# Toeplitz matrices of an S5 layer made by TensorE instead of DMA, and gate products moved ahead

## What is computed

```python
def s5_mix(u, h0r, h0i, ...):
    ...
    bu_r = jnp.einsum('btgc,gpc->btgp', uf, bbr)
    bu_i = jnp.einsum('btgc,gpc->btgp', uf, bbi)
    ...
    pr, pim, hr, hi = lax.associative_scan(_ssm_combine, (a_r, a_i, bu_r, bu_i), axis=1)
    ...
    y = (jnp.einsum('btgp,gcp->btgc', hr, c_re.astype(F32))
         - jnp.einsum('btgp,gcp->btgc', hi, c_im.astype(F32)))
    y = y.reshape(bsz, t, SEQ_WIDTH) + d_skip.astype(F32) * u.astype(F32)
    y = jax.nn.gelu(y).astype(u.dtype)
    y = y * jax.nn.sigmoid(y @ w_glu + b_glu)
```

## Time and profile before

| | |
|---|---|
| device time, median of 3 runs | 1501.69 us (1501.1 to 1504.21) |
| device time of the profiled execution | 1501.93 us |
| its span, first to last instruction | 1499.9 us |
| PE busy / PEld busy | 1408.9 us (94%) / 1309.3 us (87%) |
| DVE / ACT / POOL busy | 954.8 / 576.3 / 638.5 us |
| mean granted TensorE clock | 0.975 |

### The profile page before, as it was taken

How to read it: one execution, slowest core, us unless ns; L and a number is a source line. 1 busy time by engine, 2 the same in 40 slices (tenths; PEclk the granted TensorE clock), 3 DMA queues, 4 the chain that set the end, 5 groups by cost and what they waited for, 6 DMA issues and landing times.

```text
span 1499.9 us, 33629 instructions
## 1 busy us (share of the span) xinstructions
PE 1408.9 (94%) x12665; PEld 1309.3 (87%) x12665; DVE 954.8 (64%) x1623; ACT 576.3 (38%) x1025; POOL 638.5 (43%) x417
## 2 busy tenths in 40 slices
PE   6987868989999999999899989999999999999998
PEld 6985658979999999999889965557899999999997
DVE  5779867577773177765658688653676761377755
ACT  4554354354342134322434245431454431234323
POOL 1599322304343344442269878302214344344441
PEclk9997889999999999999999999999999999999999
DMA  6363364223333223333236669994222333223321
GB/s 175 110 139 67 66 167 127 84 59 86 98 99 99 75 84 98 91 97 91 66 109 192 204 189 313 325 328 148 75 69 85 93 96 91 84 88 94 105 83 64
DMA packets 289087, 180.55 MB, mean 120 GB/s; under 512 B 54248, under 2 KB 274572, under 8 KB 288924
## 3 DMA queue, kind: packets, MB, share of 16 engines
q1 hardware_dynamic: 288412, 179.07, 41.0%
q10 hardware_dynamic: 576, 0.13, 0.0%
HBM read 167.10 MB, written 10.63 MB: 118 GB/s over the span
## 4 chain that ended last, share of the span: by engine, by line
PE 74%; DVE 12%; issue 4%; ACT 3%; SPq 2%; DMA 2%; POOL 2%; DVEq 0%; ACTq 0%; POOLq 0%
PE big L2824 56%; PE big L2906 3%; PE misc L3021 2%; SPq L633 2%; DVE y L1869 1%; PE misc L3527 1%; DVE x L1878 1%; DVE x_lo L1320 1%; PE misc L3161 1%; PE misc L3278 1%; PE misc L3166 1%; PE misc L2891 1%; ACT w_hi L2280 1%; POOL w_lo L988 1%; PE big L2938 1%
## 5 line engine op out<-in xcount | busy, mean ns | idle before, releaser
L988 POOL TENSOR_TENSOR w_lo<-raw,w_hi 128x1024 fp32r<-128x1024 f32 (+2 forms) x150 | 387.0, 2580 | 701.7 <-ACT w_hi L2280 472.8
L2280 ACT ACTIVATE w_hi<-raw 128x1024 fp32r<-128x1024 f32 (+2 forms) x173 | 192.1, 1111 | 568.2 <-PE big L2824 536.1
L2824 PE MATMUL big<-x_hi,w_hi 128*128 128x264 f32 x1984 | 406.0, 286 | 4.7 <-DVE x_lo L1318 1.6
L2824 PE MATMUL big<-x_hi,w_lo 128*128 128x264 f32 x1984 | 400.2, 283 | 0.0
L2824 PE MATMUL big<-x_lo,w_hi 128*128 128x264 f32 x1984 | 398.2, 282 | 0.0
L2824 PEld LDWEIGHTS big<-x_hi,w_hi 128*128 128x128 f32 x1984 | 305.1, 188 | 9.5 <-issue 3.5
L2824 PEld LDWEIGHTS big<-x_lo,w_hi 128*128 128x128 f32 x1984 | 304.9, 188 | 0.0
L2824 PEld LDWEIGHTS big<-x_hi,w_lo 128*128 128x128 f32 x1984 | 304.7, 188 | 0.0
L1966 DVE SCALAR_TENSOR_TENSOR yc<-uc,convw,yc 128x512 f32<-128x512 f32 x88 | 136.7, 1553 | 113.2 <-ACT yc L2679 113.2
L2824 PE MATMUL big<-h_hi,w_hi 128*128 128x264 f32 x616 | 124.9, 284 | 6.3 <-DVE h_lo L1981 6.3
L2824 PE MATMUL big<-h_lo,w_hi 128*128 128x264 f32 x616 | 123.9, 282 | 0.0
(11 more groups left out here) (463 smaller groups left out, 2307.6 us busy)
## 6 DMA issues: line engine op xcount, KB each, us to landing
raw<-in_w_up SPq DMA_DIRECT2D x88, 512.0 KB, 3.8
raw<-in_w_down SPq DMA_DIRECT2D x32, 704.0 KB, 4.6
areas<-in_cache_k SPq DMA_DIRECT2D x41, 384.0 KB, 4.2
areas<-in_cache_v SPq DMA_DIRECT2D x41, 384.0 KB, 4.6
raw<-in_w_in SPq DMA_DIRECT2D x16, 512.0 KB, 4.4
raw<-in_w_out SPq DMA_DIRECT2D x16, 512.0 KB, 4.3
raw<-in_w_kv SPq DMA_DIRECT2D x12, 512.0 KB, 4.4
spare<-in_cache_k SPq DMA_DIRECT2D x12, 384.0 KB, 4.4
```

Of the source, the lines that this page charges most:

```text
L988: pool.tensor_tensor(w_lo[slot][:, 0:kb, :], raw[slot][:, 0:kb, :], w_hi[slot][:, 0:kb, :].bitcast(F32), ALU.subtract).then_inc(lo_made, 1)
L2280: A.activation(w_hi[slot][:, 0:kb, :], raw[slot][:, 0:kb, :], ACT.Copy).then_inc(hi_made, 1)
L2824: ins = pe.matmul(big[2 * slot + b_][:, 0:c1 - c0], w[slot][:, k, :], r[:, c0:c1], start=(k == 0 and n_ == 0), stop=(k == kb - 1 and n_ == 2))
```

## The change

1. `bb_wide` (in the idle `qrow` tile) holds each `bb` matrix with 16 zero columns on either side. With it as the stationary, TensorE forms all eight block rows of the Toeplitz matrix directly in the bank: for each 32 rows two products (odd and even block row), each as wide as the row is filled. The bank is first cleared by a product with a zero tile. ScalarE reads 128 x 512 in place of 16 x 512 straight into `toep`; `kern`, its 24 transfers and the zeroing of `toep` are gone. There are two `toep` tiles.
2. The output sums of third 0 move from third 1 to the end of third 0, ahead of head step 2. `u_load(2)` and the returns of y follow at their own waits.
3. The split parts of k = 0 to 3 go to tiles of their own (`glu_hi`, `glu_lo`), are made among the memory samples, and the products of these k for the first two panels stand right behind the output sums and the head turns, ahead of `fin_turns`. `w_lo` of these panels moves from VectorE to GpSimd, the last two adds of z from GpSimd to VectorE. Panel 2 has weight tiles of its own (`third`). The memory values (`mv0`) lie under `x_hi` and `x_lo` now, are loaded in two halves behind the load of the fourth weight panel, and `gate_in(0)` waits until they are used.

```diff
-        jobs += [("Y", 0, a) for a in range(TG // 4) if t == 1]
...
-        jobs += [("Y", 1, a) for a in range(TG // 4) if t == 1]
+        jobs += [("Y", t, a) for a in range(TG // 4) if t + 1 < THIRDS]
     for a in range(0, TG // 4, 2):
         jobs += [("mq", 0, a + b) for b in range(2)] + [("Y", THIRDS - 1, a + e) for e in range(2)]
-    jobs += [("fin", ri) for ri in range(2)] + [("OT", 0, p) for p in LAST[0]]
-    jobs += [("mq", 0, b) for b in range(TG // 4, NB)]
...
-        toep = a("toep", [P, TG, P])
+        toep = [a("toep0", [P, TG, P])]
...
-        kern = a("kern", [CH, TG, P])
+        toep.append(a("toep1", [P, TG, P]))
+        bb_wide = qrow[:, 0:2 * TP * 3 * CH].rearrange("p (r j n) -> p r j n", r=2, n=3 * CH)
...
+        third = [nc.alloc_sbuf_tensor_at(f"third_{nm}", [P, KS, P], F32R, offset=bp_end + 4 * KS * P * n)
+                 for n, nm in enumerate(("hi", "lo"))]
...
-        mb = [dict(v=a("mv0", [P, NB, 2, NMEM]), prod=a("mprod0", [P, 2, NMEM]), s_flat=a("ms0", [P, 2 * NB * MEMH + 32]),
+        glu_hi, glu_lo = (a(f"glu_{nm}", [P, KS - 2, NT], F32R) for nm in ("hi", "lo"))
+        mv0 = [nc.alloc_sbuf_tensor_at(f"mv0_{n}", [P, HALF_B, 2, NMEM], F32, offset=x_hi_at + 4 * KD * NT * n)
+               for n in range(2)]
+        mb = [dict(v=[mv0[b // HALF_B][:, b % HALF_B] for b in range(NB)], prod=a("mprod0", [P, 2, NMEM]), s_flat=a("ms0", [P, 2 * NB * MEMH + 32]),
...
-                if 0 < t < THIRDS - 1:
-                    sp.wait_ge(s_("b_used"), t + 1)
-                    sp.wait_ge(s_("cT_made"), t + 1)
-                    bc_load(t + 1)
-                if t == 1:
-                    full(sp, ("Y", 0, 3))
-                    y_store(0)
-                elif t == 2:
-                    y_return(0)
-                    full(sp, ("Y", 1, 3))
-                    y_store(1)
-                    full(sp, ("bT", 2, 3))
-                    for b in range(MK_EARLY + 1):
-                        mem_k(b)
-                    y_return(1)
-                sp.wait_ge(s_("s5_zero"), 2)
-                sp.wait_ge(s_("kern_ready"), 4 * (t + 1))
-                for tau in range(CHUNK):
-                    load(toep[CH * tau:CH * tau + CH, :, (CHUNK - 1 - tau) * CH:P],
-                         kern[:, :, 0:(tau + 1) * CH], "toep_in")
-                if t == 1:
-                    u_load(2)
-
+            sp.wait_ge(s_("b_used"), 2)
+            sp.wait_ge(s_("cT_made"), 2)
+            bc_load(2)
+            y_store(0)
+            full(sp, ("Y", 0, 3))
+            u_load(2)
+            y_return(0)
...
+            for b in range(MK_EARLY + 1):
+                mem_k(b)
...
+            def beside_glu(i):
+
+                if i != 3:
+                    return
+                sp.wait_ge(s_("yz_used"), THIRDS - 1)
+                for n in range(2):
+                    mem_v(0, mv0[n], slice(HALF_B * n, HALF_B * n + HALF_B))
+                sp.wait_ge(s_("hout_ready"), 2)
...
+            weights("glu", cols(I["w_glu"][0]), beside_glu, start=2)
...
-                        own.tell(pool.memset(toep[:], 0.0), s_("s5_zero"), 2)
-                        own.tell(pool.memset(qrow[:], 0.0), s_("s5_zero"), 3)
+                        own.tell(pool.memset(qrow[:], 0.0), s_("s5_zero"), 2)
+                        own.tell(pool.memset(zeros[:], 0.0), s_("s5_zero"), 3)
...
+                if name == "glu":
+                    for i in range(n):
+                        if i == 3:
+                            pool.wait_ge(lo_made, base + 3)
+                        if i != 2:
+                            lo(base + i, (base + i) % 2, kb)
+                    continue
...
+
+            def add_z_tile(m):
+
+                k = 2 * THIRDS - 2 + m
...
+                    dve.wait_ge(s_("yz_in"), 16 * THIRDS)
+                    dve.wait_ge(s_("yz_used"), THIRDS - 1)
+                do(V.tensor_tensor(y[:, k, :], y[:, k, :], yz_last[:, m, :], ALU.add))
+                sync()
+                mark(s_("yz_used"))
+
...
-            for b in range(4):
+            for b in range(2):
                 mem_sample(0, mb[0], b)
+            dve.wait_ge(s_("hfin_made"), THIRDS)
+            for k in range(2):
+                glu_split(k)
+            for b in range(2, 4):
+                mem_sample(0, mb[0], b)
+            for k in range(2, KS - 2):
+                glu_split(k)
+            for b in range(4, 6):
+                mem_sample(0, mb[0], b)
+            for p in LAST[0]:
+                head_lo(0, p)
+            for m in range(2):
+                add_z_tile(m)
+            glu_split(KS - 2)
             for ri in range(2):
                 full(dve, ("fin", ri))
                 freed(own, V.tensor_copy(hout[:, ri].rearrange("p a n -> p (a n)"),
                                          bank(("fin", ri))[0:108, 0:256]), ("fin", ri))
                 sync()
                 mark(s_("hout_ready"))
-            for p in LAST[0]:
-                head_lo(0, p)
...
-                    tell(V.tensor_tensor(o, srcv, h, ALU.subtract), s_("xlo_made"), stat[1] - 1 + c)
+            glu_split(KS - 1)
+            third_q = PH["glu"][2] + 2
+            dve.wait_ge(hi_made, third_q + 1)
+            dve.wait_ge(lo_made, third_q)
+            V.tensor_tensor(third[1][:], raw[third_q % 2][:, 0:KS, :], third[0][:].bitcast(F32),
+                            ALU.subtract).then_inc(lo_made, 1)
...
                 do(A.activation(y[:, k, :], y[:, k, :], ACT.Gelu_apprx_tanh))
 
+            act.wait_ge(s_("s5_zero"), 2)
             for t in range(THIRDS):
                 if t:
                     full(act, ("V", t - 1, 2))
                     input_copies(t)
-                if t == 1:
-                    read_y(0)
+                act.wait_ge(s_("b_used"), t + 1)
+                do(A.activation(bb_wide[:, :, :, CH:2 * CH], bb[t % 2][:], ACT.Copy))
+                mark(s_("bb_spread"))
...
                 for a_ in range(TG // 4):
-                    if t and a_ == 0:
-                        act.wait_ge(s_("toep_in"), 16 * CHUNK * t)
-                    read_bank(("K", t, a_), kern[:, same_side(a_)[0]:same_side(a_)[-1] + 1:2, :],
-                              bank(("K", t, a_))[0:CH, :].rearrange("p (g n) -> p g n", g=4))
-                    mark(s_("kern_ready"))
+                    read_bank(("K", t, a_), toep[t % 2][:, same_side(a_)[0]:same_side(a_)[-1] + 1:2, :],
+                              bank(("K", t, a_))[:].rearrange("p (g n) -> p g n", g=4))
+                    mark(s_("toep_ready"))
                 if t == 0:
...
                     for n in range(3, 6):
...
+            for k in range(2):
+                gelu(k)
+            sync()
+            act.wait_ge(s_("hp_ready"), THIRDS)
+            for k in range(2):
+                glu_in(k)
+            for k in range(2, KS - 2):
                 gelu(k)
             sync()
             read_y(THIRDS - 1, range(TG // 8))
+            for k in range(2, KS - 2):
+                glu_in(k)
...
+            for k in range(KS - 2, KS):
+                gelu(k)
+                sync()
                 glu_in(k)
+            act.wait_ge(raw_loaded[base % 2], ((base + 2) // 2 + 1) * 16)
+            A.activation(third[0][:], raw[base % 2][:, 0:KS, :], ACT.Copy).then_inc(hi_made, 1)
...
 
             def y_sums(t, between=None):
-                pe.wait_ge(s_("toep_in"), 16 * CHUNK * (t + 1))
...
             for t in range(THIRDS):
                 if t:
                     input_sums(t)
-                if t == 1:
-                    y_sums(0)
-                elif t == 0:
+                if t == 0:
                     pe.wait_ge(panel_read, PH["memkv1"][2] + 4)
                     scores(0, 0)
                     scores(0, 1)
+                    pe.wait_ge(s_("s5_zero"), 3)
                 pe.wait_ge(s_("cp_ready"), t + 1)
+                pe.wait_ge(s_("bb_spread"), t + 1)
                 for a_ in range(0, TG // 4, 2):
                     o = [take(("K", t, a_ + e)) for e in range(2)]
+                    for e in range(2):
+                        pe.matmul(o[e][:, :], zeros[:], ident_bf[:].unsqueeze(1).to_broadcast([P, 4, P]), start=True, stop=False)
                     for n in range(4):
                         for ri in range(2):
-                            for e in range(2):
-                                g = same_side(a_ + e)[n]
-                                r = slice(STATE * e, STATE * e + STATE)
-                                ins = pe.matmul(o[e][0:CH, n * P:n * P + P], bb[t % 2][r, ri, g // 2, :],
-                                                cp[t % 2][r, ri, g // 2, 0:P], start=(ri == 0), stop=(ri == 1))
-                                if n == 3 and ri == 1:
-                                    give(ins, ("K", t, a_ + e))
+                            for odd in (1, 0):
+                                for s in range(P // 32):
```

(66 more changed lines are left out.)

115 lines of the change are left out of this document (54 added, 61 removed).

## The result

The change makes the kernel slower. Four runs of the changed kernel took 1513.11 us in the median (1510.55 to 1519.69), four of the kernel before 1502.66 (1501.1 to 1504.21). The ratio is 1.0082, with a 95% interval of 1.0065 to 1.0100, so 12.3 us (10.5 between the medians). The forecast was 1496.6, the range 1490.5 to 1507. The time lies outside the range, on its slow side. The profiled execution of after is the slowest of its four (1519.69 us, span 1517.1, 17.2 over that of before), so its rows show some 7 us more than the median has.

The account below looks back on a forecast made before the run. A stage of dependences, no one engine the bound. +0.5 (last output bank), -6.1 (first two gate panels) and +0.5 (third) make -5.1 us on 1501.9: 1496.8, less 0.2 for the median, 1496.6 us; 80% range 1490.5 to 1507.

Parts of the forecast that it names:

- the price of the K sums: TensorE's new K sums: 8.5 us a third instead of 3.67, so +4.8 us (bounds +4.1 and +10.7).
- rival C: Slower: K records cost 25.6 ns each, 14.4 us a third, tiles not overlapped or engine underfed; 1508 us, chance 19%.
- First third: VectorE waits for scores behind the moved output sums; `cp` starts 6.2 us late, 2 more at low clock, taken as +7.5.
- Second and last third: Delay stays +7.5, last scan +3, `hp` at 203.4; ScalarE's queue then reads the last output bank at 217.2, +0.5 us.
- The 8.6 us of waiting are spent on dearer K sums: Before the last output bank: TensorE's removed waits for row loads are used up by costlier K, leaving +0.5 us.
- No wait for `toep`: Sign to look for on TensorE: its 8.6 us of waiting for the row loads disappears.
- Gate panels: Last output bank to first two finished panels: 13.3 us instead of 19.4, so -6.1 us (-5.4 to -6.8).
- Column maximum: Memory softmax behind the third gate panel: arrives 6 to 7.6 us after two panels, where 6.5 passed before; +0.5 us.
- the two terms: Last output bank to the memory softmax's column maximum: -6.1 us for the first two panels and +0.5 for the third.

Follow-up runs that it names:

- the loop: Changed kernel, three of four groups in each K bank run as one group repeated in a hardware loop (wrong sums): 1499.8 us, one run, beside 1496.9 before.
- the sums behind the third head step: Changed kernel with the first third's output sums behind the third head step, not ahead of it: ratio 1.0071; with K summed as before, 0.9984 (1498.7 us).
- the old K in the new order: Changed kernel with K summed as before, row loads included; moved output sums and gate-panel order kept: ratio 0.9968, 1497.9 us.
- the tail alone: Kernel before with only the change's last part, the early splits and first blocks of two gate panels: ratio 0.9968, 1496.8 us.
- the narrow: Changed kernel with every K product streaming 16 columns instead of 16 to 128 (K incomplete): 1518.4 us, one run, beside 1496.9 before.
- the placing products: Kernel before with only the gate-panel part, its row loads replaced by 32 selection-matrix products a third: ratio 1.0111, 1519.8 us.

## Why the prediction was wrong

**The step that failed is the first term, the price of the K sums**: 8.5 us a third, measured 13.5, 14.2 and 14.6. The working asked only whether the array overlaps its tiles. It does: 14.2 ns a record in the bursts, near the 17.5 of the earlier trace rows that I had leaned on, and 9.1 to 10.2 us for a third where the loop feeds it. What the sum left out is that 512 records with their weight loads are 1,024 instructions, four packets at 3.5 to 4 us each. The page of before gives instructions and packets; I read neither. I named the supply only inside rival C, whose price of 14.4 us was right (13.1 and 0.9 for the zeroing are 14.0; the rest is the changes of tile shape, which the text doesn't name there), and gave it 19%.

**Rival C** had the size of the term and too small a sum: 2 x 5.9 us in VectorE's chain, 1508. Measured was 1513.1. It missed that the last third's K delays the last output sums too (it ends at 224.8, 5.1 us behind `hp`), and that the output sums behind the first K then run at the low clock.

**First third.** `cp` was to be 6.2 to 7.5 us late, with a wait of 1.4 us before it; it was 17.1 late, with 8.46. The mechanism, the output sums ahead of the scores, was right. The sizes follow from K's price and from the low clock, which I had priced at 2 us and which took 4.3. With K from a loop `cp` starts at 152.01, 8.3 late. That step holds once the first is mended. That the wait should cost what it shows did not hold, as the sums behind the third head step show.

**Second and last third.** The last `hp` was forecast at 203.4. With the loop it is at 202.55, in the changed kernel at 219.64. For the last bank I let ScalarE's queue decide, 13.8 us behind `hp`; the loop kernel comes near it (15.7), but in the changed one TensorE ends its K sums at 224.8, starts the output sums at 231.89, and the bank comes 21.3 us behind `hp`. "The 8.6 us of waiting are spent on dearer K sums" understated it: the waiting was in two places, the dearer sums are in three.

**No wait for `toep`**: right.

**Gate panels.** 13.3 us from the last bank to two finished panels were forecast, 16.1 measured, 19.4 before. The last load landed 7.0 to 7.3 us after the bank (issued at 245.1, 2.8 to 3.1 in flight; 7.1 said), and the first add began at 7.55, when VectorE was free. Most of the 2.8 us too many lie behind it. The sum priced add, gelu and split for one tile (2.4 us), but two tiles pass ScalarE one behind the other, and the second one's gelu waits for the first one's split: 4.4 us from 248.46 to 252.84. The residue then stood 0.5 us behind two copies of the final states. From its end to the last product it is 2.5 us, where 1.5 and 0.7 for a low clock were allowed.

```profile
251.00 0.62 ACT L2540 ACTIVATE y<-y 128x520 f32<-128x520 f32 x1
251.65 1.19 ACT L2588 ACTIVATE x_hi<-y 128x512 fp32r<-128x512 f32 x2
```

```profile
253.35 1.15 DVE L1799 TENSOR_TENSOR x_lo<-y,x_hi 128x512 fp32r<-128x512 f32 x2 [0.18 <-DVE hout L1832]
```

**Column maximum**: +0.5 was forecast, but it came 5.4 us behind the panels where 6.5 had passed, a gain of 1.1, with a wait of 0.39 us ahead of it. Together 25.9 us became 21.4 (20.4 with the tail alone), so -4.5 to -5.5 where the two terms gave -5.6: the sum held better than its parts.

**The sum with the right price.** With the loop's K, 9 to 10 us, the column maximum is 2.95 us earlier than before, against 5.1 in the forecast. The rest of the working thus comes out within about 2 us of the trace. In device time the sign is shown by the old K in the new order, 0.9968 against 1.0082; the single run of the loop kernel (1499.8 beside 1496.9) doesn't show a gain.

The loss in the trace, changed kernel against the loop: 22.6 us at the column maximum. The K sums themselves are 12.9 of these. 4.0 are the output sums of the first third at the low clock (10.9 against 6.95 us). 3.4 are the head steps of the second third, from the end of K to the next output sums (12.7 us, 183.6 to 196.3, against 9.3, 170.5 to 179.9): the granted clock was 0.74 from 185 to 210 us in the changed kernel and 1.00 from 170 to 193 us in the loop's. The other 2.3 are not told apart. The other runs of the changed kernel are 6 to 9 us faster than the profiled one and had a mean granted clock of 0.986 to 0.989 where it had 0.979. That the clock is the reason fits, but is not shown.

The Trainium skill's page "TensorE: Matmul & The Clock Gate" (Wait — 56ns, not 53.3ns?) says start-to-start never drops below about 25 ns. The trace disagrees for tiles of 64 x 32: 162 records in 1.55 us with 16 columns, 9.6 ns each. By that rule K would have been 13 us, close to what was measured, but for a reason that the narrow and the looped kernel rule out. The same page (The mechanism) says that weight loads overlap running products only when the row group differs; the placing products, all in one row group, at 113 ns each agree with it. The four-tile products of the earlier trace rows, which share all their rows and yet pass four in 0.217 us, don't, and no run here varies the row group alone.

## What to carry to other kernels

Before a few large TensorE instructions are traded for many small ones, count the instructions, weight loads too, and divide: straight-line code was fed here at 256 in 3.5 to 4 us, so a stretch of several hundred instructions that the array could do in under some 30 ns a product and weight load waits for its own program. If it can't be avoided, put the small ones in portions (here of 512 instructions, which ran with no gap or one) between stretches of wide products, or in a loop. And when a wait of 8 us is found, ask what its engine does next before it is called a cost: here taking it away only moved it to the following operation.

## What the hardware showed that I had not expected

- Instructions are fetched in packets of some 16 KB, 256 of them, and in dense code one comes in 3.5 to 4.0 us; the engine stands 1 to 3 us between bursts, each time at the same place of the program. A loop of 128 instructions is not fetched again at each turn (71 packets against 76, two against four from 122 to 136 us, no gaps inside).
- Eight tiles of 64 x 32 overlap well: 9.6 ns a record at 16 columns, 14.2 to 15.7 at the mix of 16 to 128, 15.9 at 128 columns, which alone would be an estimated 60 ns by the 36 products of the earlier trace rows.
- Tiles of 16 rows x 32 columns in one row group with 64 to 512 columns hardly overlapped: 113 ns a record of 288 in the mean.
- A DMA issue that costs SyncE 0.72 us cost 1.38 us in the stretch where ScalarE issued too (1.02 each).
